# A transformer layer whose MLP uses Strassen steps: one ring of six places for split weights, and four Strassen steps in each of seven couples

## The reference

```python
u = rms_norm(h, norm_mix_g[0]);  h = h + nsa_mixer(u, ...)
u = rms_norm(h, norm_mlp_g[i])
h = h + jnp.square(jax.nn.relu(u @ mlp_w1[i])) @ mlp_w2[i]      # 2048 -> 8192 -> 2048
gate = jax.nn.sigmoid(rms_norm(h, ple_norm_g[i]) @ ple_w_gate[i])
h = h + gate * (p[i] @ ple_w_proj[i])
```

## Time and profile before

| | us |
|---|---|
| median of 3 runs | 1186.02 (1185.68 to 1186.06) |
| the profiled execution | 1186.18 |
| its span, first to last instruction | 1184.4 |
| TensorE, VectorE, ScalarE busy | 1176.9, 827.9, 635.5 |
| granted TensorE clock, share of full | 0.999 |

### The profile page before, as it was taken

The page is one execution under the profiler, slowest core; times in us unless marked ns, Lnnn a source line. Parts: engine busy times, 40 slices in busy tenths (PEclk is TensorE's granted clock), DMA queues, the critical chain, the costliest instruction groups (busy, mean ns, idle before and its releaser), DMA issues.

```text
span 1184.4 us, 14269 instructions
## 1 busy us (share of the span) xinstructions
PE 1176.9 (99%) x5417; PEld 978.0 (83%) x5417; DVE 827.9 (70%) x1141; ACT 635.5 (54%) x882; POOL 22.5 (2%) x31
## 2 busy tenths in 40 slices
PE   9999999999999999999999999999999999999998
PEld 7888888888888888888888888888888888888886
DVE  5568876888776667755788755879655888676554
ACT  6745455666656565543565543456533566455443
POOL 1000100000000000000000000000000000000000
PEclk9999999999999999999999999999999999999999
DMA  9867663333348665865477865476854577886661
GB/s 341 322 178 242 215 235 139 108 108 134 109 162 281 210 215 199 279 233 194 146 244 250 273 214 191 176 247 232 285 195 178 192 243 241 273 258 208 217 207 44
DMA packets 110980, 249.26 MB, mean 210 GB/s; under 512 B 9664, under 2 KB 55744, under 8 KB 110912
## 3 DMA queue, kind: packets, MB, share of 16 engines
q1 hardware_dynamic: 110768, 248.34, 61.9%
q10 hardware_dynamic: 144, 0.01, 0.0%
HBM read 233.63 MB, written 14.68 MB: 210 GB/s over the span
## 4 chain that ended last, share of the span: by engine, by line
PE 99%; DMA 0%; DVE 0%; SPq 0%; ACT 0%; issue 0%
PE acc L1786 59%; PE acc L1812 11%; PE tr L1812 7%; PE sc L1786 7%; PE sc L1812 6%; PE sc L2013 1%; PE sc L1978 1%; PE tr L1930 1%; PE tr L1919 0%; PE sc L1919 0%; PE tr L2066 0%; PE tr L2065 0%; DMA w_raw<-in_nsa_w_in_units_dram 0%; PE acc L1902 0%; PE tr L2042 0%; PE tr L2043 0%
## 5 line engine op out<-in xcount | busy, mean ns | idle before, releaser
L1176 DVE TENSOR_TENSOR w_split<-w_raw,w_split 128x1024 fp32r<-128x1024 f32 x296 | 358.7, 1220 | 211.6 <-ACT w_split L733 210.9
L733 ACT ACTIVATE w_split<-w_raw 128x1024 fp32r<-128x1024 f32 x296 | 309.7, 1057 | 255.3 <-PE acc L1786 194.3
L1786 PE MATMUL acc<-w_split,b_split 128*128 128x512 f32 x1536 | 355.3, 390 | 0.0
L1786 PEld LDWEIGHTS acc<-w_split,b_split 128*128 128x128 f32 x1536 | 287.3, 188 | 59.1
L1786 PE MATMUL acc<-w_split,a_hi 128*128 128x512 f32 x1020 | 318.1, 393 | 1.6 <-DVE w_split L1172 1.6
L1786 PEld LDWEIGHTS acc<-w_split,a_hi 128*128 128x128 f32 x1020 | 188.6, 188 | 40.9 <-issue 2.4
L1786 PE MATMUL acc<-w_split,a_lo 128*128 128x512 f32 x510 | 198.9, 390 | 0.0
L744 ACT ACTIVATE w_split<-w_raw 128x1024 fp32r<-128x1024 f32 x95 | 97.6, 1052 | 44.4 <-PE acc L1786 20.9
L1190 DVE TENSOR_TENSOR w_split<-w_raw,w_split 128x1024 fp32r<-128x1024 f32 x78 | 93.3, 1217 | 31.3 <-ACT w_split L744 31.3
L1786 PEld LDWEIGHTS acc<-w_split,a_lo 128*128 128x128 f32 x510 | 95.7, 188 | 20.3
L1812 PE MATMUL acc<-w_split,a_hi 128*128 128x512 f32 x298 | 91.7, 389 | 0.0
(11 more groups left out here) (253 smaller groups left out, 1091.3 us busy)
## 6 DMA issues: line engine op xcount, KB each, us to landing
w_raw<-in_mlp_w_units_dram SPq DMA_DIRECT2D x256, 512.0 KB, 4.4
w_raw<-in_nsa_w_in_units_dram SPq DMA_DIRECT2D x76, 512.0 KB, 4.6
w_raw<-in_nsa_w_out_units_dram SPq DMA_DIRECT2D x32, 512.0 KB, 4.2
w_raw<-in_ple_w_gate_units_dram SPq DMA_DIRECT2D x32, 512.0 KB, 4.3
turn_dram<-s SPq DMA_DIRECT2D x52, 128.0 KB, 3.4
turn_dram<-junk SPq DMA_DIRECT2D x44, 128.0 KB, 3.5
v_slc<-turn_dram SPq DMA_DIRECT2D x22, 256.0 KB, 3.8
v_win<-turn_dram SPq DMA_DIRECT2D x22, 256.0 KB, 4.6
```

Source lines behind the costliest of these rows:

```text
L733: nc.scalar.activation(w_hi[:, u % SPLIT], w_raw[:, u % RAW], ACT.Copy).then_inc(hi_done, 1)
L1176: nc.vector.tensor_tensor(w_lo[:, u % SPLIT], w_raw[:, u % RAW], f32(w_hi[:, u % SPLIT]), ALU.subtract).then_inc(lo_done, 1)
L1786: last = nc.tensor.matmul(banks_of(c)[t][:], xs[:, kt, toks], ws[:, u % SPLIT, m * NW:(m + 1) * NW], start=(kt == 0 and n == 0), stop=(kt ...
```

## The change

- `QUADS` is (3, 4, 5, 6) in all seven couples. `combined_rows` and the split of `r_raw` become four steps long; the split's high part moves from the block before into unit 0 of the first couple, its low part from unit 0 to unit 1.
- Everything split is an item in one order: each unit, and behind a step's second unit two items for the sums (T1, T3) and (T2, T4). Items take places in a ring: of four up to the first Strassen unit, of six from there to the end of the kernel (the two further places are `t_split`).
- The sums go into `t_raw`, out of place: one 1024-column addition (B11 + B12 and B22 + B12), then two of 512. They stand ahead of the first unit's low part and wait for the raw units alone. `w_raw` is left as it is, so a raw slot is free after its own unit's low part.
- TensorE takes a step's items one after the other and gives each place back by itself.
- Work between the units moves by one unit (`pair_sums` and `add_to_h` from s == 2 to 3, `turn_hidden` from 4 and 6 to 5 and 7, ScalarE's and SP's with it). Blocks are turned in place (`row_turned = row_blocks`), with a wait for the set two before. The load and split of `p` move from the last output block of the attention to the last down block.

```diff
-QUADS = (2, 4, 6)
+QUADS = (3, 4, 5, 6)
...
-    return QUADS if (c - C_MLP) % 8 == 0 else QUADS[1:]
+    return QUADS
...
+def _number_items():
+    n = 0
+    for u in range(UNITS + 1):
+        ITEM[u] = n
+        n += 1
+        if u - 1 in QUAD_UNITS:
+            T_ITEM[u - 1] = (n, n + 1)
+            n += 2
+    return n
...
+WIDER = ITEM[QUAD_UNITS[0]]
+PLACES = (SPLIT, SPLIT + 1, *((WIDER + n) % SPLIT for n in range(SPLIT)))
+
+def place(item):
+    return item % SPLIT if item < WIDER else PLACES[(item - WIDER) % len(PLACES)]
+
+def place_free(item):
+    if WIDER <= item < WIDER + len(PLACES) - SPLIT:
+        return 0
+    return item + 1 - (SPLIT if item < WIDER else len(PLACES))
...
-        row_blocks = (junk[:], key_blocks)
-        row_turned = [v[:].rearrange("p t n -> p (t n)") for v in (v_slc, v_win)]
+        row_turned = row_blocks = [v[:].rearrange("p t n -> p (t n)") for v in (v_slc, v_win)]
...
+        def weights(item):
+            n = place(item)
+            return (x[:, n % SPLIT] for x in ((w_hi, w_lo) if n < SPLIT else (t_hi, t_lo)))
...
-                    sp.wait_ge(lo_done, raw_free(u - RAW))
+                    sp.wait_ge(lo_done, ITEM[u - RAW] + 1)
...
+            def place_hi(item, src, at=0):
+                if place_free(item):
+                    act.wait_ge(unit_used, place_free(item))
+                hi, _ = weights(item)
+                nc.scalar.activation(hi[:, at:UW], src, ACT.Copy).then_inc(hi_done, 1)
...
+                    if u - 1 in QUAD_UNITS:
+                        place_hi(ITEM[u], w_raw[:, u % RAW, NW:UW], NW)
+                        for m, item in enumerate(T_ITEM[u - 1]):
+                            act.wait_ge(sums, 3 * QUAD_UNITS.index(u - 1) + 2 * m + 1)
+                            place_hi(item, t_raw[:, m])
...
+            def place_lo(item, src, at=0):
+                dve.wait_ge(hi_done, item + 1)
+                hi, lo = weights(item)
+                nc.vector.tensor_tensor(lo[:, at:UW], src, f32(hi[:, at:UW]), ALU.subtract).then_inc(lo_done, 1)
+
+            def weight_sums(u):
+                at, n = QUAD_UNITS.index(u), u % RAW
+                blocks_of = w_raw[:, n:n + 2].rearrange("p u (m j) -> p (u m) j", m=2)
+                b22 = w_raw[:, n + 1, NW:UW]
+                t2, t4 = (t_raw[:, 1, m * NW:(m + 1) * NW] for m in range(2))
+                dve.wait_ge(raw_full[n], 16 * (u // RAW + 1))
+                dve.wait_ge(raw_full[n + 1], 16 * (u // RAW + 1))
+                if at:
+                    dve.wait_ge(lo_done, T_ITEM[QUAD_UNITS[at - 1]][1] + 1)
+                nc.vector.tensor_tensor(t_raw[:, 0].rearrange("p (m j) -> p m j", m=2), blocks_of[:, 0:4:3],
+                                        blocks_of[:, 2:3].broadcast_to([P, 2, NW]), ALU.add).then_inc(sums, 1)
+                dve.wait_ge(sums, 3 * at + 1)
+                nc.vector.tensor_tensor(t2, t_raw[:, 0, 0:NW], b22, ALU.add).then_inc(sums, 1)
+                dve.wait_ge(sums, 3 * at + 2)
+                nc.vector.tensor_tensor(t4, t2, w_raw[:, n, NW:UW], ALU.add).then_inc(sums, 1)
...
             def split_lo_pair(c):
                 for s in range(2 * UPC):
                     u = FIRST[c] + s
...
+                    if u in QUAD_UNITS:
+                        weight_sums(u)
+                    if u - 1 in QUAD_UNITS:
+                        place_lo(ITEM[u], w_raw[:, u % RAW, NW:UW], NW)
+                        for m, item in enumerate(T_ITEM[u - 1]):
+                            place_lo(item, t_raw[:, m])
+                    else:
+                        place_lo(ITEM[u], w_raw[:, u % RAW])
                     yield s
...
-                        if s == 2:
+                        if s == 3:
                             pair_sums(c - 2)
-                        if s in (4, 6):
+                        if s in (5, 7):
                             turn_hidden(n + s // 2 - 2)
...
+                pe.wait_ge(lo_done, own[0] + 1)
+                product(one, tile_rows(2 * k, 0), split(own[0], 0), start, stop)
+                product(c11, tile_rows(2 * k + 1, 0), split(own[0], 1), False, False).then_inc(unit_used, 1)
+                pe.wait_ge(lo_done, own[1] + 1)
                 pe.wait_ge(r_done, 1)
+                product(c12, combined(3), split(own[1], 1), False, False).then_inc(unit_used, 1)
+                pe.wait_ge(lo_done, rest[0] + 1)
+                product(five, combined(0), split(rest[0], 0), start, stop)
+                product(seven, combined(2), split(rest[0], 1), start, stop).then_inc(unit_used, 1)
+                pe.wait_ge(lo_done, rest[1] + 1)
+                product(six, combined(1), split(rest[1], 0), start, stop)
+                product(c21, tile_rows(2 * k + 1, 1), split(rest[1], 1), False, False).then_inc(unit_used, 1)
```

More of the change, by code:

```diff
@@ L224, in trunk_layer @@
             pass
[L225 to L229, removed]
+        with nc.sbuf_tensor("t_split", [P, 2, 2, UW], F32R) as t_split:
+            with nc.sbuf_tensor("t_raw", [P, 2, UW], F32) as t_raw, \
+                    nc.sbuf_tensor("r_split", [P, 2, 4, N_QUADS, P], F32R) as r_split, \
+                    nc.sbuf_tensor("mixed", [P, 4, NW], F32) as mixed:
+                pass
+            with nc.sbuf_tensor("p_raw", [P, 2, SEQ], F32) as p_raw, \
+                    nc.sbuf_tensor("pt_hi", [P, 2, SEQ], F32R) as pt_hi, \
+                    nc.sbuf_tensor("pt_lo", [P, 2, SEQ], F32R) as pt_lo:
+                pass
         t_hi, t_lo = t_split[:, 0], t_split[:, 1]
@@ L741, in split_hi_pair @@
                     act.wait_ge(raw_full[u % RAW], 16 * (u // RAW + 1))
[L742 to L756, removed]
+                    if u == QUAD_UNITS[0]:
+                        act.wait_ge(r_done, 1)
+                    if u - 1 in QUAD_UNITS:
[4 more added lines that the diff above has]
+                    else:
+                        place_hi(ITEM[u], w_raw[:, u % RAW])
                     yield s
@@ L1073, in up_pair @@
                     if p and not q:
+                        if s == 0:
+                            act.wait_ge(r_ready, 1)
+                            nc.scalar.activation(r_hi, r_raw[:], ACT.Copy).then_inc(r_rounded, 1)
                         if s == 1:
@@ L1784, in tile_product @@
                 m, toks = kt % UNIT_KT, slice(t * P, (t + 1) * P)
[L1785 to L1787 removed]
+                hi, lo = weights(ITEM[u])
+                for n, (xs, ws) in enumerate(((x_hi, hi), (x_hi, lo), (x_lo, hi))):
+                    last = nc.tensor.matmul(banks_of(c)[t][:], xs[:, kt, toks], ws[:, m * NW:(m + 1) * NW],
                                             start=(kt == 0 and n == 0), stop=(kt == KT - 1 and n == 2))
@@ L1817, in tile_rows, with split @@
                 return tuple(x[:, kt, t * P:(t + 1) * P] for x in (a_hi, a_lo))
+            def split(item, m):
+                return tuple(x[:, m * NW:(m + 1) * NW] for x in weights(item))
             def plain_unit(u, k, half, banks):
-                pe.wait_ge(lo_done, u + 1)
+                pe.wait_ge(lo_done, ITEM[u] + 1)
                 for m in range(UNIT_KT):
                     kt = UNIT_KT * k + m
-                    w = tuple(x[:, u % SPLIT, m * NW:(m + 1) * NW] for x in (w_hi, w_lo))
+                    w = split(ITEM[u], m)
                     for t in range(TT):
@@ L1832, in quad @@
                 u = FIRST[c] + 2 * k
-                at = QUAD_UNITS.index(u)
-                def split(x, v, m):
-                    return tuple(y[:, v, m * NW:(m + 1) * NW] for y in x)
+                own, rest = (ITEM[u], ITEM[u + 1]), T_ITEM[u]
                 def combined(r):
                     return tuple(x[:, r, i] for x in (r_hi, r_lo))
-                own, sums_of = (w_hi, w_lo), (t_hi, t_lo)
                 start, stop = k == quads(c)[0], k == quads(c)[-1]
```

152 lines of the change are left out of this document (55 added, 97 removed).

## The result

| | us |
|---|---|
| before, median of 4 runs | 1185.85 (1185.18 to 1186.06) |
| after, median of 4 runs | 1196.59 (1196.01 to 1198.19) |
| ratio | 1.0094, 95% interval 1.0079 to 1.0108 |
| the profiled execution after; its span | 1198.19; 1196.5 |

The change made the kernel 10.7 us slower. The sign and the mechanism were as forecast; the size was 6.5 us in the forecast, and the time lies just over the range's upper end. The page of the kernel after, against the earlier trace rows: TensorE has 33 matmuls fewer and the chain is no longer its own alone.

A forecast was written before the change was run, and what follows sets the result against it. TensorE, busy 99%, was taken as the bound, fed by VectorE in the couples. Profiled run 1186.18 - 7.48 for matmuls + 14.0 of new waits = 1192.7, as median 1192.5 us; range 1188.0 to 1196.5.

The forecast's parts named there:

- Matmuls removed, 7.48: TensorE in the couples: 11 more Strassen steps lose 3 matmuls each, 33 in all, 7.48 us less.
- VectorE's step, 6.61: VectorE's work in one Strassen step, sums and low parts: 6.61 us against TensorE's 4.76, so 1.85 behind per step.
- TensorE's handoff, 0.1: From VectorE's ready piece to TensorE at a Strassen step: 0.1 us added, an estimate.
- First couple 1.1, left 1.1, right 3.2: TensorE's new waits per couple in us: quarter 0's; first of quarters 1 to 3; second of quarters 1 to 3.
- Where they stand: TensorE's waits: right couples at third and fourth step, some 3 us; others at the fourth, about 1.
- The anchors: Start points of VectorE's chain in each couple kind; in right couples it leaves the mixing 2.12 us ahead of TensorE.
- No ring or buffer shortens it.: Right couples: VectorE never waits in their chain, so no ring or buffer shortens it; 3.2 us late each.
- Rival 1: Couples: no wait comes, TensorE stays the bound, 1178.5 us; with double sum at 0.69, 1181.8; both together chance 0.12.
- Rival 2: Couples: only part of the waits, anchors 1 us too late; right 2.2, others 0.1; 1185.5 us; chance 0.06.
- Rival 3: Down block: the lag goes on, 1 to 3 us in three or four quarters, 1196 to 1202; chance 0.06.
- Rival 4: VectorE in three couples: each operation at full duration, 0.08 us more for 59, 10.9 in all: 1203; chance 0.01.
- The rest at nothing: Sums' own buffer, ring outside the couples, moved splits, blocks turned in place, later SP turns: each worth 0 us.

The follow-up runs named there:

- e2: Changed kernel, 28 steps, without the two 512-column sums of each step on VectorE (output not the layer's): 1177.44 us, ratio to before 0.9929.
- e5: Changed kernel with e3's waits and 24 Strassen steps: 2, 4, 6 in first couple, 2, 3, 4, 6 in left, 3, 4, 6 in right: 1180.19 us.
- e6: Changed kernel with e3's waits and 24 Strassen steps: 3, 5, 6 in first and right couples, 1, 3, 5, 6 in left: 1180.58 us.
- e9: Changed kernel with e3's waits, 24 steps: 3, 5, 6 in first couple, 1, 3, 5 in left, 1, 3, 5, 6 in right: 1180.27 us.
- e3: Changed kernel with the double sum waiting only for the low part before the one directly ahead; the second sum takes the other wait: 1194.59 us.
- e10: As e9, but steps 1, 3, 6 instead of 1, 3, 5 in left couples, still 24 steps: 1198.55 us, ratio to before 1.0109.
- e8: Changed kernel with steps 4 and 6 alone in left couples, four steps in first and right ones (22 steps): 1195.55 us.
- e1: Changed kernel with the 17 Strassen steps of before; new ring, sums' own buffer, turns in place and moved work stay: 1185.04 us, ratio 0.9993.
- run 17: Not a run's label: "run" is a verb here, 17 is us. The 25-step kernel meant, changed kernel with e3's waits, took 1179.36 us.
- e4: Changed kernel with e3's waits and the weights' three sums moved from VectorE to GpSimd; raw slots wait for them: 1234.52 us, ratio 1.0410.

## Why the prediction was wrong

The mechanism was right, and a size was off: the sum of the new waits, 14.0 us in the forecast, is 18.5. Two terms made it so. VectorE's step was priced without its wait on the last low part (2.8 of the 4.5 us), and the handoff to TensorE was 0.26 short in each couple (1.8 us).

- *Matmuls removed, 7.48.* Right: 5384 matmuls, and e2, e5, e6 and e9 gain the pitch of what they leave out.
- *VectorE's step, 6.61.* Mis-sized: up to 6.82. The double sum 1.22, the pitches of the parts and the order were right. What I put at nothing is the new wait of the double sum on the previous step's last low part. The description of the change says that the sums wait for the raw units alone, but its own diff has this wait (`lo_done`), and the prediction has no term for it. That low part is the operation directly ahead, and without a wait the next start overlaps the end before it (1.14 for 1.22). The wait costs 0.2 per step. It counts three times in the first couple (0.6), twice in a left one (0.4), and comes to 0.3 in a right one, whose second step follows transposes: 2.8 us in all. e3 moves it and gets 2.0 us back.
- *TensorE's handoff, 0.1.* The time from VectorE's double sum to TensorE's matmul was right (641.36 to 645.23, 3.87 for 3.91). Two things were not in it, once per couple. I took a couple's zero from the chain, where a piece begins at the end of the record before it, 0.15 behind the first matmul's start. And the first matmuls behind a wait come 0.11 slower. Together 0.26, 1.8 us in seven couples. A right couple's first wait adds nothing to its lateness, since its second wait is shorter by as much.
- *First couple 1.1, left 1.1, right 3.2.* Measured, idle time and 0.26 at each wait: 1.65 + 0.26 = 1.9, 1.46 + 0.26 = 1.7, 3.29 + 0.52 = 3.8. Together 1.9 + 5.2 + 11.4 = 18.5; 18.5 - 7.48 = 11.0 for a measured 10.7. The first couple's first matmul begins 0.35 us earlier than before (438.56 for 438.91), which no term of mine had.
- *Where they stand.* Right in all ten cases. The anchors, too: VectorE leaves the mixing 2 us ahead of TensorE, and e9 against e10 shows that the end of the left couple's last step sets this lead. e8 shows that the left couple's number of steps doesn't.
- *"No ring or buffer shortens it."* Right for the right couples as they are. But I took the place of the mixing as given, and e9 shows that it can be moved at no cost in matmuls.
- *Rival 1* (no wait) is what e2 shows with VectorE's load taken away; its point of decision, 5.5 us per step, isn't contradicted by e2's 5.36, which costs no wait. *Rival 2* didn't happen: right couples wait more than the forecast, not less. *Rival 3* didn't happen: no wait stands in a down block. *Rival 4*, by the rule of the Trainium skill's "VectorE: DVE Perf Modes" (Terms, DRAIN), gave 1203. Between independent operations the rows go on against it (four of 1024 columns end in 4.62, 1.13 apart), but behind a wait the full duration is paid and 0.04 to 0.13 more (1.22 to 1.26; 2.48 for two low parts), and it was such a wait that I missed.
- *The rest at nothing.* Right: e1.
- *The granted clock.* Not in the forecast. In the profiled execution one fall of 3.4 us at half, worth 1.6 us. How often the other runs have it isn't shown, so the cause of 1196.0 against 1198.2 is only argued. The miss doesn't rest on it: the 18.5 us leave it out.

The range's upper end took 0.4 per right couple for the double sum and 1 us for all handoffs. The time lies 0.1 us above it, so the miss is small beside what the two terms were off. It would have held had the wait been seen and priced from its nearest row: VectorE's 0.73 against 0.60, for the same kind of wait, was in the earlier trace rows, and gives some 2 us as an estimate (0.13 for each of about 17 steps).

## What to carry to other kernels

Where a fast engine is fed by a slower one in bursts, add up the feeder's work from its last forced wait to each piece that is wanted, and compare the two clocks there; shares of busy time (70% here) don't tell. The cheap cures are to spread the heavy steps, to let the forced wait (here the mixing behind a couple's last Strassen step) come earlier, and to take a few steps less: 25 steps, spread and with the looser wait, run 17 us faster than 28 (15 us faster than 28 with the looser wait). Price every wait on the same engine's last write, and what TensorE loses behind a wait, as terms of their own, and read the waits from the diff, not from its description.

## What the runs showed of the hardware

- Behind a wait of TensorE three matmuls of 512 columns need 0.57 us for two pitches instead of 0.46 (645.23 to 645.80, 642.62 to 643.08).
- Two VectorE operations with a wait between them begin 0.12 to 0.21 us further apart than without: 1.26 against 1.14 behind 1024 columns, 0.73 against 0.60 behind 512, and 2.48 against 2.27 from two low parts to the double sum (the changed kernel and e3).
- GpSimd adds 1024 float32 columns in 3.09 us and 512 in 1.8 to 2.0 while VectorE works, and two of VectorE's operations with two operands go from 2.36 to 5.12 us beside it (e4).
- In each of e10's three waits of 3.9 us the granted clock fell to half (1.2 GHz) before TensorE went on, and cost 6.7 us behind them. Behind two waits of 1.5 and 1.8 us close together it fell so in one of the changed kernel's three right couples, and in none of e3's or e8's, in the profiled executions.
